# A decoder step on one core: x on two queues first of all and a narrow dt block, state additions ahead of convolutions, weight blocks of sample turns begun ahead of row pages

## The reference, cut to what matters

```python
cq, ckv_raw, kr_raw, z, xbc, dt_raw, mq, g_raw = _split_in(x @ w_in)
o_mla = latent attention (prompt: causal; sample: over 16 cached pages of 128 tokens per sequence)
xbc   = silu(causal depthwise conv of 4 taps over xbc)
dt    = softplus(dt_raw + dt_bias)                       # 32 heads
S     = S * exp(last)[..., None, None] + einsum('bjgh,bjgn,bjghp->bghpn', wb, Bc, xc)
y     = within-chunk part + C S * exp(cum) + d_skip * xs # then times silu(z), grouped RMS norm
o_mem = 4-head cross attention into 256 memory tokens
m  = sig(gA)*(o_mla@WoA) + sig(gB)*(o_ssm@WoB) + sig(gM)*(o_mem@WoM);  x1 = LN(alpha*x + m@w_out)
out = LN(alpha*x1 + relu(x1@w_up+b_up)^2 @ w_down + b_down)
```

## Time and profile before

| | |
|---|---|
| time, median of 3 runs (lowest to highest) | 1900.84 us (1896.15 to 1905.06) |
| profiled execution, time and span | 1905.42 us, span 1903.8 us |
| mean granted TensorE clock | 0.962 of 2.4 GHz |
| TensorE busy, matmuls | 1768.7 us, 93% of the span |
| VectorE / ACT / GpSimd busy | 36% / 20% / 19% |
| chain that ended last | PE 84%, DVE 5%, DMA 4%, SP's queue 3% |
| HBM read, rate over the span | 190.08 MB, 108 GB/s |

### The profile page before, as it was taken

One profiled execution on the slowest core, in us unless ns is written; L12 is line 12 of the kernel. 1 busy time (PEld: TensorE's weight loads), 2 busy tenths in 40 slices (PEclk: granted clock), 3 DMA queues, 4 the chain that ended last, 5 costly groups with the idle time before them and its releaser, 6 DMA issues.

```text
span 1903.8 us, 25271 instructions
## 1 busy us (share of the span) xinstructions
PE 1768.7 (93%) x10220; PEld 1458.4 (77%) x10220; DVE 677.9 (36%) x1228; ACT 374.9 (20%) x737; POOL 360.9 (19%) x314
## 2 busy tenths in 40 slices
PE   7999989999999999999989799999994999999995
PEld 5766757667787778776767577778893999999994
DVE  4555657556341121112111112312214770167103
ACT  1151422514312121111101011100014111111112
POOL 0030131311310000000222210000032434444340
PEclk9998989989999999999989899999996999999998
DMA  4422324223243222223566664422220222232211
GB/s 161 148 78 79 128 67 146 82 79 130 93 150 132 65 67 67 67 78 104 179 221 192 207 221 181 168 100 78 89 67 19 82 89 78 89 89 89 78 56 47
DMA packets 70407, 206.59 MB, mean 109 GB/s; under 512 B 10162, under 2 KB 26675, under 8 KB 65683
## 3 DMA queue, kind: packets, MB, share of 16 engines
q1 hardware_dynamic: 48656, 148.72, 24.0%
q10 hardware_dynamic: 15490, 35.28, 5.1%
q0 software_dynamic: 6144, 20.98, 3.5%
HBM read 190.08 MB, written 14.86 MB: 108 GB/s over the span
## 4 chain that ended last, share of the span: by engine, by line
PE 84%; DVE 5%; DMA 4%; SPq 3%; ACT 2%; issue 2%; ACTq 0%; POOL 0%; DVEq 0%; POOLq 0%
PE acc L1528 35%; PE acc L1575 23%; PE acc L1801 6%; PE acc L1767 2%; DMA ring<-in_stream 2%; PE bank L1711 2%; SPq L558 1%; PE acc L1749 1%; SPq L560 1%; DVE work L1054 1%; PE bank L1556 1%; PE bank L1816 1%; PE bank L1835 1%; PE bank L1817 1%; PE bank L1888 1%
## 5 line engine op out<-in xcount | busy, mean ns | idle before, releaser
L1528 PE MATMUL acc<-xt,ring 128*128 128x272 f32 x2496 | 622.9, 409 | 28.8 <-DMA ring<-in_stream 28.8
L1528 PEld LDWEIGHTS acc<-xt,ring 128*128 128x128 f32 x2496 | 487.4, 198 | 158.8 <-issue 57.5
L1575 PE MATMUL acc<-x_parts,f_parts 128*128 128x272 f32 x1664 | 233.4, 291 | 24.4 <-POOL f_parts L481 24.4
L481 POOL TENSOR_TENSOR f_parts<-ring,f_parts 128x1024 fp32r<-128x1024 f32 x72 | 174.4, 2422 | 403.6 <-ACT f_parts L638 403.5
L1575 PEld LDWEIGHTS acc<-x_parts,f_parts 128*128 128x128 f32 x1664 | 220.5, 191 | 25.1 <-issue 24.8
L1575 PE MATMUL acc<-f_parts 128*128 128x272 f32 x1536 | 197.3, 290 | 6.2 <-DVE mark L1493 6.2
L1575 PEld LDWEIGHTS acc<-f_parts 128*128 128x128 f32 x1536 | 195.5, 190 | 7.1 <-DVE mark L1493 6.7
L459 POOL DMA_DIRECT2D work<-in_page_cols x128 | 69.0, 539 | 501.3 <-PE bank L1856 392.2
L638 ACT ACTIVATE f_parts<-ring 128x1024 fp32r<-128x1024 f32 x72 | 76.5, 1062 | 372.2 <-PE acc L1575 366.3
L1801 PE MATMUL acc<-branch,ring 128*128 128x272 f32 x512 | 120.0, 392 | 0.0
L1801 PEld LDWEIGHTS acc<-branch,ring 128*128 128x128 f32 x512 | 96.0, 190 | 18.8
(11 more groups left out here) (304 smaller groups left out, 1820.4 us busy)
## 6 DMA issues: line engine op xcount, KB each, us to landing
ring<-in_stream SPq DMA_DIRECT2D x217, 512.0 KB, 3.5
work<-in_page_cols POOLq DMA_DIRECT2D x128, 160.0 KB, 2.7
attended<-in_ssm_state ACTq DMA_DIRECT2D x8, 1024.0 KB, 7.6
work<-cum_rows SPq DMA_DIRECT2D x32, 256.0 KB, 4.6
out_ssm_s<-attended ACTq DMA_DIRECT2D x8, 1024.0 KB, 6.2
work<-in_ckv_rows ACTq DMA_DIRECT2D x64, 128.0 KB, 3.2
work<-in_ckv_rows SPq DMA_DIRECT2D x64, 128.0 KB, 2.6
work<-in_memk_cols SPq DMA_DIRECT2D x8, 1024.0 KB, 6.4
```

The lines of the kernel that those rows point to most:

```text
L481: pool.tensor_tensor(split[j][1], ring[:, s * BLOCK:(s + 1) * BLOCK], split[j][0].bitcast(F), SUB).then_inc(sem["split_ready"], 1)
L1528: m = pe.matmul(acc[p][:, half, 0:width], w[:, k * P:(k + 1) * P], x(kk)[:, half * width:(half + 1) * width], start=kk == 0, stop=kk == n_ ...
L1575: m = pe.matmul(acc[p][:, half, 0:HT], w[:, k * P:(k + 1) * P], x[:, kk, of], start=kk == 0 and n == 0, stop=kk == n_blocks * KC - 1 and n ...
```

## The change

It has three parts, in five places of the code, and a change of the stream on the host.

1. *Start.* The dt block keeps only its 32 real output columns: SP loads 128 x 256 of it (128 KB instead of 512), and TensorE's 16 matmuls use 32 columns of weights each. They go chunk by chunk now, both halves of the tokens for each. SP issues the four even chunks of x right behind the dt block, ahead of block 1 and the constants; ACT issues the four odd ones. The constants come between block 1 and the others, as they did between block 0 and the others.
2. *State stage.* VectorE's pairs of `add_state` move up, each ahead of the convolution that stood before it.
3. *Sample stage.* SP loads five blocks behind the row pages of turn 0 and three behind those of each later turn (one behind the last), where it loaded three ahead of each turn's pages and three at the end.

```diff
+            dt_cols = KC * SSM_HEADS
+            sp.dma_start(ring[:, 0:dt_cols], stream[0][:, 0:dt_cols]).then_inc(sem["weights_in_slot0"], 16)
+            block_at.next()
+            for c in range(0, KC, 2):
+                sp.dma_start(X[:, c, :], x_t[:, c, :]).then_inc(sem[f"x{c // 2}_loaded"], 16)
             load()
             sp.dma_start(cst[:, :], const).then_inc(sem["const_loaded"], 16)
-            load(QC - 1)
+            load(QC - 2)
...
             cached_rows(0)
+            load(5)
             for b in range(1, DEC_BATCH):
-                load(3)
                 cached_rows(b)
-            load(3)
+                load(3 if b < DEC_BATCH - 1 else 1)
...
-            for c in range(KC):
+            for c in range(1, KC, 2):
                 act.dma_start(X[:, c, :], x_t[:, c, :]).then_inc(sem[f"x{c // 2}_loaded"], 16)
...
                 weigh(7)
+                add_state(0)
+                add_state(1)
                 ahead(2)
                 ahead_finish(1)
-                add_state(0)
-                add_state(1)
+                add_state(2)
+                add_state(3)
                 read_y(2)
...
-            for half in range(2):
-                for k in range(KC):
-                    if half == 0 and k % 2 == 0:
-                        pe.wait_ge(sem[f"x{k // 2}_loaded"], 32)
-                    m = pe.matmul(acc[0][:, half, 0:HT], w[:, k * P:(k + 1) * P], X[:, k, half * HT:(half + 1) * HT],
-                                   start=k == 0, stop=k == KC - 1)
+            for k in range(KC):
+                if k % 2 == 0:
+                    pe.wait_ge(sem[f"x{k // 2}_loaded"], 32)
+                for half in range(2):
+                    m = pe.matmul(acc[0][0:SSM_HEADS, half, 0:HT], w[:, k * SSM_HEADS:(k + 1) * SSM_HEADS],
+                                  X[:, k, half * HT:(half + 1) * HT], start=k == 0, stop=k == KC - 1)
```

More of the change, by code:

```diff
@@ L1234, in _ @@
                 gate_y(2)
-                add_state(2)
-                add_state(3)
+                add_state(4)
+                add_state(5)
                 ahead(3)
                 ahead_finish(2)
-                add_state(4)
-                add_state(5)
                 read_y(3)
@@ L1243, in _ @@
                 gate_y(3)
+                add_state(6)
+                add_state(7)
                 ahead(4)
                 ahead_finish(3)
-                add_state(6)
-                add_state(7)
                 ahead(5)
@@ L2040, in lay_out @@
     add = lambda x: blocks.extend(x.reshape(-1, P, BLOCK))
-    dtp = np.zeros((D_MODEL, P), np.float32); dtp[:, :SSM_HEADS] = dt
-    add(tiles(dtp))
+    dtp = np.zeros((P, BLOCK), np.float32)
+    dtp[:, :KC * SSM_HEADS] = dt.reshape(KC, P, SSM_HEADS).transpose(1, 0, 2).reshape(P, KC * SSM_HEADS)
+    add(dtp)
     tx, tz = tiles(xbc), tiles(z)
```

## The result

The changed kernel takes 1828.18 us, the median of four runs (1827.66 to 1828.4), against 1902.95 for the kernel before, also of four (1896.15 to 1908.82). The ratio is 0.9608, its 95% interval 0.9574 to 0.9642. I had predicted 1834, with a range of 1823 to 1856.

A forecast was written before the change was run, and what follows sets the result against it. TensorE, busy 93% of the span and 84% of the chain, was taken as the bound. 1905.4 - 1.4 - 27.8 - 40.5 = 1835.7, or 1831 if 4.6 us between profile and median lie elsewhere; predicted 1834, range 1823 to 1856.

The forecast's parts named there:

- a dt block that is cold throughout: Start: all 32 dt records at the lower clock, 0.458 us each, ending at 20.2 against 23.2; gain 1.4 us.
- The rival's upper end: Start: narrow matmuls warm the clock, block ends at 14.9; gain 8.3 instead of 1.4, total 1827; chance 0.20.
- State stage: State additions read ahead of convolutions: gain 27.8 us, 13.8 of waits and 14.0 of clock.
- The small second wait: State stage: TensorE's remaining wait for state additions, 1.1 us, goes as well.
- Sample stage: Weight blocks ahead of row pages: gain 40.5 us over turns 1 to 7, 26.3 of waits and 14.2 of clock.
- a turn without either is 25.77: Sample stage: turn 4's 28.77 us without its wait of 2.77 and 0.23 of slowness is 25.77 us.
- The key pages: Sample stage rival: key pages arrive last, a wait of 2.0 a turn; 1848 at half of the full price 27; chance 0.16.
- I price this at nothing, with 1.5 us of cover: Sample stage: last key page lands at 24.3 of a 25.8 us turn, so key pages cost nothing.
- the gap of the earlier trace: Sample stage, GpSimd's page issue: POOL once stood 3.15 us between two issues in the kernel before.
- its slower rival: Sample stage: GpSimd's page issue stretches in the new overlap, four of sixteen steps every turn; 1909 us; chance 0.03.
- the main case: Whole kernel: the forecast of 1834 us, in a band of 1828 to 1841; chance 0.52.

The follow-up runs named there:

- the fourth kernel: Changed kernel plus VectorE reading sample outputs ahead of the convolution and two turn-0 weight blocks ahead of that turn's row pages: 1811.72 us, ratio 0.9544.

## Why the prediction was right, and which step of it failed

**Start: the step that failed.** "I therefore take a dt block that is cold throughout." It gained 8.1 us and not 1.4. The transfers were as computed: TensorE started at 5.59 (5.5 predicted), and the block never stalled. But 32 records took 9.6 us, not 14.7. I had read the cold stretch behind line 1711 as the mark of a quarter-full array and took 32 columns for 32 rows. The 32-row block is cold to its end, the 32-column block is as fast as the 128-column one. The rival's upper end, 14.9 for block 1, is what came (15.16). As the prediction had it, the earlier x came from what x is put ahead of: one queue does as well.

**State stage: right.** 26.7 us a group in two of three, and a slack of 0.9 us for additions 2 and 3 where 1 had been worked out. The small second wait went too: outside the groups the stretch from block 1 to the heads fell from 387.91 to 382.89 us, of which 1.1 are this wait, and the other 3.9 are stretches of low clock that had not stood in the sum. They come and go between executions and are luck as much as gain. Against them group 2 kept 2 us more than the others. In all it is 29.7 where 27.8 were predicted. The run that moves only the first pair shows that the move of the later ones was hardly needed: without it only 1.1 us of waits come back.

**Sample stage: right in the mechanism, 2.6 us short in size.** The weight blocks' waits are gone in turns 1 to 7 and the clock stayed at 1.00. The term "a turn without either is 25.77" measured 25.96, 1.3 us in seven turns. Turn 4 of before had been taken as slow by 0.23 and was slow by 0.04, so most of that slowness belongs to any turn. The key pages cost 2.05 us, once: that rival was right about who comes next and wrong about how often. "I price this at nothing, with 1.5 us of cover" held at the start of six turns of seven, with 1.5 to 2.0 us of cover behind turns 1 to 5. What it left out is the gap of the earlier trace rows: the prediction used it only in its slower rival, four times a turn, and not once in the main case, where it takes 2.5 us out of a cover of 1.5. That would be a wait of about 1 us; a landing of 4.4 us instead of 3.3 made it 2.05. SP's pages did begin 18.4 us into the turn (18.2 predicted), and GpSimd's issue did not stretch in the overlap: the one gap of 3.15 us is where it was before. With that the slower rival falls. Turn 0 gave back 0.9 by a block that happened to be warm.

**The sum.** 8.1 + 29.7 + 1.7 + 37.9 + 0.4 = 77.8 us against 69.7. The difference is the dt block (+6.7), the low-clock stretches outside the groups and among the heads (+1.9 and +1.7), the turns and the key pages (-2.6), and 0.4 in the rest. The time, 1828.2, is 6 us from the 1834 predicted, and the warm dt block alone is 6.7: the main case had the start wrong, and the case that came true there had been given 1827. That the rest fits so closely is in part luck, as misses of 2 to 3 us stand on both sides.

**What stays open.** Why GpSimd stands 3.15 us at the same page load in every kernel (3.15 to 3.17 in all twelve traces), why the last page then took 4.4 us to land, and why additions with 128 rows and the half block behind them take 0.28 us less than with 32. Which of the fourth kernel's two moves gives how much was read from its marks; they weren't run apart.

## What to carry to other kernels

When TensorE makes up most of the chain, as here with 84%, look early at the order within each engine's and each queue's program: all three gains came from putting what is needed next ahead of something that waits or isn't due, and the narrower dt block, the only work that was saved, added nothing that could be told from none. Price such a wait with the clock behind it: the low clock was 14 of the 28 us predicted for the state stage, and they came. Look at every irregular step of a trace too, even one that costs nothing yet: GpSimd's one gap became a wait when the turns grew shorter. The runs of the kernel lay 13 us apart before and 0.7 after, but 4 in the fourth experiment, and what sets this spread is not shown. When you take a row as a witness for an operation that the trace does not have, ask in which property the two agree: rows and columns of a matmul tile are not the same thing.

## What the runs showed of the hardware that I had not expected

- In this kernel the rows that a matmul used made a difference to the granted clock, and the columns did not. At the start, 32 records of 128 rows and 32 columns took 9.63 us and rose to full clock; 32 records of 32 rows and 128 columns took 14.84 and stayed at the lower level of 1.2 GHz. Behind 2.10 us of idling, four matmuls of 32 rows left the next half block cold (5.62 us), four of 128 rows left it warm (3.83). Without the idling, four of 32 rows left it warm too (3.93).
- The same wait may or may not cost the clock: in turn 0, a wait of 3.33 us was followed by a warm block (7.57) in the changed kernel, and 3.2 us by a cold one (9.20) in the run with one block ahead.
- Beside SP's row pages, the last key page of a turn took 2.9 to 3.4 us to land; in the kernel before, where those pages came later, 2.4 to 2.6 us.
- GpSimd's one gap of 3.15 us between page loads stands at the second load of turn 6 in the kernel before and in the changed one, though it comes 67 us earlier in the span (1017.96 and 1085.30).
